# Stage boundaries split by halves of the tokens, in a six-stage decoder trunk of fp32 matmuls

## The reference

```python
x = x + 0.5 * _rmsnorm(_swiglu(_rmsnorm(x, ng[0]), w_in, w_out), ng[1])
h = _rmsnorm(x, ng[2])
x = x + _rmsnorm(mixer(h), ng[3])
x = x + 0.5 * _rmsnorm(_swiglu(_rmsnorm(x, ng[4]), w_in, w_out), ng[5])
```

## Time and profile before

| | us |
|---|---|
| three runs: median (lowest, highest) | 2353.21 (2351.65, 2354.58) |
| profiled execution, its own time | 2352.79 |
| span of its instructions | 2351.1 |
| PE busy | 2274.0 (97%), 11226 matmuls |
| PE weight loads busy | 1855.6 (79%) |
| DVE busy | 1239.0 (53%) |
| ACT busy | 982.3 (42%) |
| GpSimd busy | 422.4 (18%) |
| mean granted TensorE clock | 0.987 of full speed |

### The profile page before, as it was taken

The page is one execution under the profiler, slowest core; times in us unless marked ns, Lnnn a source line. Parts: engine busy times, 40 slices in busy tenths (PEclk is TensorE's granted clock), DMA queues, the critical chain, the costliest instruction groups (busy, mean ns, idle before and its releaser), DMA issues.

```text
span 2351.1 us, 31330 instructions
## 1 busy us (share of the span) xinstructions
PE 2274.0 (97%) x11226; PEld 1855.6 (79%) x11226; DVE 1239.0 (53%) x1490; ACT 982.3 (42%) x1403; POOL 422.4 (18%) x323
## 2 busy tenths in 40 slices
PE   8999998999999999999999998899999999999999
PEld 7888886788778888878888886677788887888887
DVE  5445336666555454345545338776655644645423
ACT  5322334555543223334232336565566643432312
POOL 2112101111122121012212002123721102112100
PEclk9999999999999999999999999899999999999999
DMA  5333332222223332332332332122112222443341
GB/s 163 106 89 91 90 96 71 81 75 76 63 63 115 90 98 79 97 101 90 98 98 74 104 90 91 48 72 64 60 58 82 64 90 72 117 115 90 104 146 63
DMA packets 84719, 207.92 MB, mean 88 GB/s; under 512 B 25088, under 2 KB 29312, under 8 KB 84640
## 3 DMA queue, kind: packets, MB, share of 16 engines
q1 hardware_dynamic: 84640, 206.85, 29.1%
HBM read 202.56 MB, written 4.26 MB: 88 GB/s over the span
## 4 chain that ended last, share of the span: by engine, by line
PE 87%; DVE 6%; ACT 3%; POOL 2%; issue 1%; DMA 0%; DVEq 0%; SPq 0%; ACTq 0%; POOLq 0%
PE bank L1787 68%; PE bank L2031 7%; PE bank L1837 5%; DVE h_lo L1067 1%; POOL gd_o L1710 1%; DVE resid L1082 1%; DVE w_lo L1063 1%; POOL sq L1707 1%; DVE y L1077 1%; PE bank L2193 1%; PE bank L2200 1%; ACT w_hi L571 0%; ACT h_hi L595 0%; PE bank L1992 0%; PE bank L2172 0%
## 5 line engine op out<-in xcount | busy, mean ns | idle before, releaser
L1063 DVE TENSOR_TENSOR w_lo<-raw,w_hi 128x1024 fp32r<-128x1024 f32 x395 | 571.8, 1465 | 513.6 <-ACT w_hi L571 513.4
L1787 PE MATMUL bank<-h_hi,w_hi 128*128 128x512 f32 x1720 | 685.3, 398 | 38.8 <-DVE h_lo L1067 32.1
L1787 PE MATMUL bank<-h_hi,w_lo 128*128 128x512 f32 x1720 | 675.7, 393 | 0.0
L1787 PE MATMUL bank<-h_lo,w_hi 128*128 128x512 f32 x1696 | 666.1, 393 | 0.0
L571 ACT ACTIVATE w_hi<-raw 128x1024 fp32r<-128x1024 f32 x395 | 415.4, 1055 | 563.4 <-PE bank L1787 470.0
L1787 PEld LDWEIGHTS bank<-h_hi,w_hi 128*128 128x128 f32 x1720 | 326.8, 190 | 116.4 <-issue 33.2
L1787 PEld LDWEIGHTS bank<-h_hi,w_lo 128*128 128x128 f32 x1720 | 326.4, 190 | 69.7
L1787 PEld LDWEIGHTS bank<-h_lo,w_hi 128*128 128x128 f32 x1696 | 322.4, 190 | 68.7 <-issue 3.1
L1651 POOL TENSOR_TENSOR y<-y,up 128x512 f32<-128x512 f32 x88 | 173.1, 1967 | 744.2 <-DVE up L1106 670.1
L1106 DVE TENSOR_TENSOR up<-bank,rms 128x512 f32<-128x512 f32 x88 | 60.7, 690 | 351.3 <-PE bank L1787 351.3
L1787 PE MATMUL bank<-act_hi,w_hi 128*128 128x512 f32 x528 | 205.4, 389 | 0.0
(11 more groups left out here) (277 smaller groups left out, 2632.5 us busy)
## 6 DMA issues: line engine op xcount, KB each, us to landing
raw<-in_ffn_in SPq DMA_DIRECT2D x172, 512.0 KB, 3.7
raw<-in_gd_in SPq DMA_DIRECT2D x49, 512.0 KB, 3.6
raw<-in_ffn_out SPq DMA_DIRECT2D x48, 384.0 KB, 3.1
raw<-in_hg_in SPq DMA_DIRECT2D x32, 512.0 KB, 3.6
raw<-in_ffn_out SPq DMA_DIRECT2D x48, 320.0 KB, 2.9
raw<-in_last_out SPq DMA_DIRECT2D x22, 512.0 KB, 3.6
raw<-in_gd_out SPq DMA_DIRECT2D x16, 512.0 KB, 3.7
raw<-in_hg_out SPq DMA_DIRECT2D x8, 512.0 KB, 3.5
```

The lines of the kernel that those rows point to most:

```text
L1063: nc.vector.tensor_tensor(w_lo[:, r, :], raw[:, r, :], w_hi[:, r, :].bitcast(f32), ALU.subtract).then_inc(lo_split, 1)
L1787: ins = nc.tensor.matmul(dst, w, moving[ml][:, k, :], start=first and n == 0 and (wl, ml) == (0, 0), stop=last and n == len(ks) - 1 and wl ...
```

## The change

The last output tile of a stage, and the first four chunks of the boundary and of the head start, are done in two halves of 256 tokens. The list `ITEMS` orders the boundary's work: chunks 0 to 3 in half 0 (items 0 to 3), chunks 0 to 3 in half 1 (items 4 to 7), then chunks 4 to 7 whole (items 8 to 11). The output sum is done once for each half, the first of them in the midst of the last tile's second half. The root of half 1 is made by ACT after h_hi of item 3. ACT's squares of the input go to a tile of their own, `x_sq`, whole chunks, square c after h_hi of item c+4. GpSimd adds all eight of them (seven adds), so that the input sum of stages 1 to 5 is one matmul of ones. That sum comes after the head start (HGRN2 and DeltaNet) or after unit 4 (FFN). DVE's splits of the next stage's first four units move from the out-tile loop into the boundary: one before item 0, the others before `scale` of items 1, 2 and 3. The diff, cut to its core:

```diff
+        ITEMS = [(c, 0) for c in range(SPLIT)] + [(c, 1) for c in range(SPLIT)] + [(c, 2) for c in range(SPLIT, KD)]
+        def pre_sums(s):
+            return 3 * s + 1
+        def post_sums(s, h):
+            return 3 * s + 2 + h
...
             def pre(s):
...
+                    high(s, 2)
+                    high(s, 3)
+                    root(post_sums(s - 1, 1), 1, half(1))
+                    for i in range(SPLIT, N_ITEMS):
+                        high(s, i)
+                        square(i - SPLIT)
                 split((first_unit[s] + RING, 0))
-                root(2 * s)
+                root(pre_sums(s), 0, half(2))
...
+                for q in range(RING - n_u, RING - 3):
+                    split((w0 + q, 0))
+                act.wait_ge(half_made, s + 1)
+                act.wait_ge(acc_done, POOLED * (2 * s + 1) + POOLED - 1)
+                last_half(0)
+                root(post_sums(s, 0), 1, half(0))
+                if n_u == 4:
+                    split((w0 + 1, 0))
+                high(s + 1, 0)
+                if n_u > 1:
+                    split((w0 + 2, 0))
+                high(s + 1, 1)
+                act.wait_ge(unit_used, w0)
+                last_half(1)
+                split((w0 + 3, 0))
...
             def boundary(s):
...
+                split((first_unit[s], 0))
                 scale(0)
                 add(0)
+                for i in range(N_ITEMS):
+                    if i < RING - 1:
+                        split((first_unit[s] + i + 1, 0))
+                    if i + 1 < N_ITEMS:
+                        scale(i + 1)
+                    low(s, i)
+                    if i + 1 < N_ITEMS:
+                        add(i + 1)
...
                 def pair(u, n, b, first=False):
                     if first:
                         split(ahead(u, 4))
-                        dve.wait_ge(rms_ready, 2 * s + 1)
+                        dve.wait_ge(rms_ready, pre_sums(s))
...
-                with dve.Fori(0, n_out if s < LAST - 1 else n_out - RING, RING) as i:
+                with dve.Fori(0, n_out - RING, RING) as i:
...
-                sum8(2 * s)
+                if s == 0:
+                    sum8(0)
+                for c in range(1, KD if s else 0):
+                    pool.wait_ge(sq_done, SQUARES * s + c + 1)
...
+                    nc.gpsimd.tensor_tensor(acc[:], x_sq[:, 0, :] if c == 1 else acc[:], x_sq[:, c, :], ALU.add).then_inc(acc_done, 1)
...
             def head_start(s):
...
+                for i in range(SPLIT - 1):
+                    for q in range(RING - 1):
+                        chunk(i, q)
+                        if i == 0 and q == 1:
+                            sum_outputs(s - 1, 1)
+                for i in range(SPLIT - 1):
+                    chunk(i, RING - 1)
+                for i in range(SPLIT - 1, N_ITEMS):
                     for q in range(RING):
+                        chunk(i, q)
+                if kinds[s] != "ffn":
+                    sum_inputs(s)
...
                         blocks(bank[banks[q]][:], u, 0, (h_hi, h_lo), range(KD), True, True).then_inc(unit_used, 1)
+                        if s and banks[q] == 5:
+                            sum_inputs(s)
...
+                def last_tile(u):
+                    alone = 1 if n_u == 4 else 0
+                    turns = [(q, h) for q in range(alone) for h in range(2)] + [(q, h) for h in range(2) for q in range(alone, n_u)]
+                    for q, h in turns:
+                        pe.wait_ge(lo_split, u + q + 1 + SKEW)
+                        ks = range(cuts[q], cuts[q + 1])
+                        dst = bank[7 - h][:]
+                        if (q, h) == (alone, 1):
+                            blocks(dst, (u + q, 0), 0, moving, ks[:2], q == 0, False, h)
+                            sum_outputs(s, 0)
+                            ins = blocks(dst, (u + q, 0), 2, moving, ks[2:], False, q == n_u - 1, h)
...
```

More of the change, by code:

```diff
@@ L94, in trunk @@
         upper = sb("upper", [P, P])
+        with nc.sbuf_tensor("x_sq", [P, KD, TOK], f32) as x_sq:
+            pass
         with ExitStack() as region:
@@ L398, in __getitem__ @@
                 i = head_order.index(at[1])
-                return go_hi[:, i, :] if i < EARLY else h_hi[:, i - EARLY, :]
+                return go_hi[:, i, :] if i < EARLY else h_hi[:, KD - VH + i, :]
         class Lows:
@@ L571, in split @@
                 nc.scalar.activation(w_hi[:, u[0] % RING, :], raw[:, u[0] % RING, :], ACT.Copy).then_inc(hi_split, 1)
[L573 to L583, removed]
@@ L585, in pre, with root @@
-            def pre(s):
[L586 to L594, removed]
+            def root(n, which, cols):
+                act.wait_ge(sum_ready, n)
+                nc.scalar.activation(rms[:, which, cols], bank[4][:, cols], ACT.Ln, bias=eps, scale=1.0 / D).then_inc(rms_logged, 1)
+                act.wait_ge(rms_logged, n)
+                nc.scalar.activation(rms[:, which, cols], rms[:, which, cols], ACT.Exp, scale=-0.5).then_inc(rms_ready, 1)
@@ new lines, in high, with square @@
+            def high(s, i):
+                c, h = ITEMS[i]
+                act.wait_ge(x_ready, N_ITEMS * (s - 1) + i + 1)
+                nc.scalar.activation(h_hi[:, c, half(h)], x[:, c, half(h)], ACT.Copy, scale=pre_gain(s, c)).then_inc(h_hi_ready, 1)
+            def square(c):
+                nc.scalar.activation(x_sq[:, c, :], x[:, c, :], ACT.Square).then_inc(sq_done, 1)
+            def pre(s):
+                for c in range(KD if s == 0 else 0):
+                    cols = slice(c * P, (c + 1) * P)
+                    act.wait_ge(first_loaded[c], 32)
+                    nc.scalar.activation(w_hi[:, :, cols], raw[:, :, cols], ACT.Copy).then_inc(hi_split, 1)
+                    act.wait_ge(const_loaded, N_CONST)
+                    act.wait_ge(const_made, 3)
@@ L651, in out_tiles @@
                 tiles = RING // n_u
+                per = max(tiles, 2)
                 v0 = first_unit[s] + IN_UNITS[kinds[s]]
[L654 to L669, removed]
@@ L670, in out_tiles, with tile @@
-                step = max(tiles, 2) // tiles
+                def tile(i, t):
+                    u = (v0 + t * n_u, 4 * i) if not isinstance(i, int) else (v0 + 4 * i + t * n_u, 0)
+                    c = tiles * i + t
+                    for q in range(n_u - 1):
+                        split(ahead(u, 4 + q))
+                    act.wait_ge(unit_used, count(u) + n_u)
+                    wait(act, acc_done, POOLED * (2 * s + 1) + c - 1)
+                    nc.scalar.activation(sq[:, t % 2, :], bank[t % 2][:], ACT.Square).then_inc(sq_done, 1)
+                    wait(act, y_scaled, N_ITEMS * s)
+                    nc.scalar.activation(m[:, bass.ds(c, 1), :].rearrange("p a n -> p (a n)"), bank[t % 2][:], ACT.Copy).then_inc(m_copied, 1)
+                    split(ahead(u, 3 + n_u))
@@ L671, in out_tiles, with last_half @@
+                def last_half(h):
+                    nc.scalar.activation(sq[:, POOLED % 2, half(h)], bank[7 - h][:, half(h)], ACT.Square).then_inc(sq_done, 1)
+                    nc.scalar.activation(m[:, KD - 1, half(h)], bank[7 - h][:, half(h)], ACT.Copy).then_inc(m_copied, 1)
+                step = per // tiles
                 n = KD // tiles
                 act.preload_act_table_set("natural_log_exp_and_others")
-                with act.Fori(0, n - step, step) as i:
-                    four(i)
@@ L675, in out_tiles @@
-                four(n - step, s == LAST - 1)
-                root(2 * s + 1)
+                if n > 2 * step:
+                    with act.Fori(0, n - step, step) as i:
+                        for t in range(per):
+                            tile(i, t)
+                else:
+                    for t in range(per):
+                        tile(0, t)
+                for t in range(per - 1):
+                    tile(n - step, t)
+                w0 = first_unit[s + 1]
+                for q in range(RING - n_u, RING - 3):
+                    split((w0 + q, 0))
@@ L1869, in out_proj, with four @@
                 v0 = first_unit[s] + IN_UNITS[kinds[s]]
-                def four(i, peeled=False):
+                def four(i, peeled=False, last=False):
                     for t in range(max(tiles, 2)):
```

147 lines of the change are left out of this document (91 added, 56 removed).

## The result

The changed kernel takes 2380.34 us (median of four runs, 2379.80 to 2381.59), the kernel before beside it 2352.43. The ratio is 1.012, with a 95% interval of 1.0104 to 1.0136: **slower by 1.2%, 27.9 us**. The forecast was 2373, and slower at 0.80. The result lies in the range, and 7 us above the number.

What follows compares the result with a forecast made beforehand. DVE was taken to set the pace inside the head start, PE being busy nearly throughout. Input sum in HGRN2 and DeltaNet 1.4, in FFNs 17.9, clock 1.0: +20.3 on 2352.79, said as 2373 us; range 2353 to 2388.

Steps and rivals of the forecast that it cites:

- The sum behind unit 4: FFN heads at boundaries 2, 3, 5: moving the input sum there delays unit 6 by 7.3, 5.4 and 5.2, 17.9 us.
- the clock behind its stalls: FFN heads: slow PE clock after the waits behind the moved input sum, 0.3 us for each FFN, 1 in all.
- The PE idle after it: FFN, after the input sum: PE waits for w_lo of unit 5, able to go on 4.15 us after the sum.
- The half matmul: PE's 256-column matmul in the last tile and half chunks: taken at 0.120 us, ends 0.113 and 0.190.
- the rival of the weight loads: Weight loads set the half matmul's pace: 2387 us at 0.150 each, 2412 at 0.190; chance 0.10.
- The first y: After an FFN, at T-2.2, 5.7 us earlier; T is the old start of the stage output's sum over partitions.
- DVE's chain: Boundary, from the first y to the end of the last h_lo: 30.2 us, against 24.4 before.
- half operations: DVE operations on 256 columns in the boundary: about 0.48 us each, 0.27 less than whole.
- the root: DVE's wait for the second root, made by ACT after h_hi of item 3: 1.5 us with hops.
- holds: DVE operations kept waiting by GpSimd's adds, six of them among items 5 to 11: 6.5 us, ends 0 and 7.6.
- clock in the head start: Rival: PE gaps at items 2, 6 and 8 slow its clock, 1.3 us at five boundaries, 2380 us; chance 0.15.
- The faster rival: PE keeps its own pace in the head start, all h_lo in time: 2343 us; chance 0.09.

Runs made afterwards that it cites:

- before_pe_sums: Kernel before, whole chunks, with PE adding up the input's squares in eight matmuls by ones and no GpSimd input add: 2357.07 us, ratio 1.0017.
- before_wlo_inside: Kernel before, with the four w_lo splits of the next stage's first units placed between the head start's chunks in DVE's queue: 2371.42 us, ratio 1.0077.
- adds_one_only: Changed kernel, with only the first GpSimd input add whole, those of chunks 2 to 7 cut to 8 columns: 2361.56 us, ratio 1.0047.
- before_adds_one_only: Kernel before, with GpSimd's input adds of chunks 2 to 6 cut to 8 columns: 2350.50 us, ratio 0.9996.

## Why the prediction was right, and where it was short

*Right, by its own reasons.* The sum behind unit 4 was to cost 17.9, and 1.0 more for the clock behind its stalls; undone it gave 17.8 in all, added to the kernel before it cost 17.9 in all. The PE idle after it was to be 4.15, then unit 6 to start 11.15 after the sum's end (after boundary 3 this is 1090.69, 1089.83 and two matmuls of 0.43): unit 5 starts at 1094.74 and unit 6 at 1101.96, 4.05 and 11.3. The half matmul was taken at 0.120, and is 0.120 in these rows, which settles the rival of the weight loads. The rule of the Trainium skill, "TensorE: Matmul & The Clock Gate", section "Back-to-back issue gap", would have it at 109 ns; the trace has more, as it had for whole ones. The first y was to come at T-2.2 after an FFN: boundary 1 shows 368.99, which with the shift of 0.44 is T-2.1.

*DVE's chain* was to be 30.2; it is 30.67, 29.95, 30.69, 30.69, 30.29. Its terms hold one by one: half operations 0.48; the root 1.39 and a hop for the 1.5; holds 6.25 for the 6.5 (two on halves and four on whole operations at boundary 1, each 1.0 to 1.1). The rule of the Trainium skill, page "SBUF — State Buffer", section "SBUF: two separate sides", agrees with the trace for halves: 1.52 where 0.48 is the free time, so that the half is held as long as the whole.

*Short by 7.* The sum of the parts was +20.3, the spans show +27.5. The largest term that was put too small is the clock in the head start, which the sum had at nothing. After the last h_lo, "PE then has 0.14 plus 12 x 0.227", which is 2.86 us. Where the clock stayed full, that held: at boundary 4 the last h_lo ends at 1456.91 and the input sum begins 2.92 later:

```profile
1456.16 0.75 DVE L1118 SCALAR_TENSOR_TENSOR h_lo<-resid,gain_table,h_hi 128x512 fp32r<-128x512 f32 x1 [0.79 <-ACT h_hi L603]
...
1459.83 1.02 PE L1842 MATMUL bank<-acc,ones 128*128 128x512 f32 x2
```

At boundary 1 it begins 4.06 later (399.65 to 403.71), since PE had run for 3.4 us at half clock:

```profile
391.90:395.30 3.40, 3.40 (x10) 2.62 (x9) 3.27 (x4) 1.42 (x3) 1.32 (x1) 0.51 0.00 0
```

That is a window of the changed kernel, granted clock 0.51, right behind the wait of 2.24 at 391.10. It happened in the head starts of boundaries 1, 2 and 5, and cost 1.1 each. This is the rival called clock in the head start, which had 0.15 and 2380; I doubted it for one short wait of 0.23 that could not speak for a wait of 2.24. That its 2380 is the measured time is luck in part: it supposed five slow stretches of 1.3, and three of 1.1 came. The other terms are small. The chains are 1.3 longer than 30.2, all five together; 1.0 is a slow stretch in HGRN2; 0.8 arises in DeltaNet and 0.4 ahead of the first boundary; the last half microsecond was not settled.

*Wrong, though it cost nothing here:* "since there DVE, not PE, sets the pace", and with it the reading of the earlier trace rows as two waits at each boundary. The ten waits for h_lo are one of 7.28 at the kernel's start, one of 4.69 ahead of each of the five head starts, and only four inside them, 1.38 us in all:

```profile
7.28 0.77 PE L1787 MATMUL bank<-h_hi,w_hi 128*128 128x512 f32 x1 [7.28 <-DVE h_lo L1067]
...
390.33 0.50 PE L1787 MATMUL bank<-h_hi,w_hi 128*128 128x512 f32 x1 [0.23 <-DVE h_lo L1067]
...
396.48 0.50 PE L1787 MATMUL bank<-h_hi,w_hi 128*128 128x512 f32 x1 [0.39 <-DVE h_lo L1067]
...
1062.34 0.50 PE L1787 MATMUL bank<-h_hi,w_hi 128*128 128x512 f32 x1 [0.38 <-DVE h_lo L1067]
...
1998.06 0.50 PE L1787 MATMUL bank<-h_hi,w_hi 128*128 128x512 f32 x1 [0.38 <-DVE h_lo L1067]
```

The head starts of boundaries 2 and 4 have none. In the kernel before, the two engines ended together. Up to the input sum PE took 22.65 us at boundary 1, and with the chain 4.8 shorter still 21.45; and with a chain of 18.05 (before_pe_sums) nothing more came of it. A count of 21.8 for 96 matmuls against 24.4 hid that PE starts 3.2 after the first y and runs at half clock behind its 4.69 of idleness: 3.2 + 19.75 + 1.7 and the last nine matmuls are 26.7 after the first y, level with DVE's 24.4 plus the last chunk's twelve, 27.1 (the input sum between them left out of both). This is why cutting the same GpSimd adds gained 18.8 us in the changed kernel and nothing in the one before. With the early y, PE's bound moves ahead and DVE's chain is left as the bound; what stands in it is then paid, until PE's own pace is reached again.

*The faster rival* ("items 4 to 11; it needs holds gone, halves at half cost and the second root early") had its place right. Given the early root and no holds, and the sum kept where its wait is covered, the kernel is 18 us faster than before, although a half operation costs 0.48 and not half of 0.75. Its number, 2343, can't be set against the measured 2334: it held the price of the sum's place, which this kernel does not pay, and not PE's eight matmuls a boundary, which it does. The change itself had none of the three.

## What to carry to other kernels

Before a bound is shortened, ask what would have ended the same stretch without it: here two engines ended together, and the early start paid off only when the other engine's queue was cleared as well. List the waits one by one before calling an engine the bound: a total of 32.1 us hid that only 1.38 of it lay in the stretch in question. And when a run comes out at the forecast time, look whether the wait that the forecast named is in its trace; in before_wlo_inside it was not. When a small reduction is moved off the busy engine's last covered place, follow every queue that waits for its result, for the work behind that wait is what becomes late, not the result. An experiment that mends one wait should be read for where the next one falls, and for the clock behind it.

## What the runs showed of the hardware

A wait of PE of the same 2.24 us, in the same place and for the same operation, was followed by 3 us at a granted clock of 0.52 in one kernel and 1.00 in another; in the changed kernel it was so at three of five boundaries. What decides it was not found. After waits of 0.38 and 0.42 ahead of items 6 and 8 (adds_one_only, boundary 1) it stayed at 1.00.

A GpSimd add of only 8 columns was listed at 0.76 to 0.77 us in three of five cases at boundary 1 of before_adds_one_only, among DVE's operations, and at 0.20 and 0.24 in the two others. Its columns did not set its length, since all five have eight; the timeline of this kernel, GpSimd:

```profile
387.49 0.76 POOL L1632 TENSOR_TENSOR sq<-sq 128x8 f32<-128x8 f32 x1 [1.38 <-ACT sq L576]
389.63 0.20 POOL L1632 TENSOR_TENSOR sq<-sq 128x8 f32<-128x8 f32 x1 [1.38 <-ACT sq L576]
```
